# Second block's feed-forwards: normalised inputs of 256 columns from the fifth unit on, 112 bytes off the weights

## The reference, cut to what matters

```python
h = _modulate(_rmsnorm(x, ffn1_norm[l]), sh1, sc1)          # h * (1 + scale) + shift
x = x + FFN_RES * gt1[:, None, :] * _swiglu(h, ffn1_w_in[l], ffn1_w_out[l])
# _swiglu: a, b = split(h @ w_in); (silu(a) * b) @ w_out     D_FF = 2816
```

## Time and profile before

| | |
|---|---|
| median of 3 runs | 3090.3 us (3087.77 to 3093.15) |
| profiled execution, its own time | 3091.63 us |
| its span | 3089.9 us, mean granted clock 0.99 |
| PE / PEld / DVE / ACT / POOL busy | 97% / 87% / 68% / 31% / 23% |
| outer units of FF0 to FF3 | 134.0, 135.1, 133.9, 131.6 us |
| inner units of FF0 to FF3, first to last matmul's start | 63.7, 63.0, 63.5, 62.2 us |

### The profile page before, as it was taken

How to read it: one execution, slowest core, us unless ns; L and a number is a source line. 1 busy time by engine, 2 the same in 40 slices (tenths; PEclk the granted TensorE clock), 3 DMA queues, 4 the chain that set the end, 5 groups by cost and what they waited for, 6 DMA issues and landing times.

```text
span 3089.9 us, 45987 instructions
## 1 busy us (share of the span) xinstructions
PE 3001.7 (97%) x18914; PEld 2685.3 (87%) x18914; DVE 2103.8 (68%) x2247; ACT 971.1 (31%) x1027; POOL 703.3 (23%) x614
## 2 busy tenths in 40 slices
PE   8999999999999999999998899999999999999999
PEld 5778889988887888878888699899989999999999
DVE  4864359867279543795637776687797868768764
ACT  2112222212131121221215343343544343354443
POOL 1220100124113010130201022231462313228110
PEclk9999999999999999999999999999999999999999
DMA  7543235322245333353623387586547868755564
GB/s 266 191 150 96 95 87 200 137 96 82 96 127 192 126 94 103 123 204 109 204 99 123 107 268 251 172 279 225 200 158 247 258 204 274 239 188 198 158 188 154
DMA packets 501665, 522.74 MB, mean 169 GB/s; under 512 B 15732, under 2 KB 433830, under 8 KB 501478
## 3 DMA queue, kind: packets, MB, share of 16 engines
q1 hardware_dynamic: 498536, 513.76, 50.4%
q0 software_dynamic: 2944, 6.32, 1.0%
HBM read 518.97 MB, written 1.05 MB: 168 GB/s over the span
## 4 chain that ended last, share of the span: by engine, by line
PE 77%; DVE 15%; ACT 3%; issue 3%; DMA 2%; POOL 0%; SPq 0%; DVEq 0%; ACTq 0%
PE ps L2309 22%; PE ps L2396 15%; PE ps L2486 14%; PE ps L2337 7%; PE ps L2510 7%; DVE wl L1293 4%; DVE acc L1247 3%; PE ps L2374 2%; DVE lnp L1247 2%; ACT wh L864 2%; PE ps L2353 2%; PE ps L2423 1%; DVE mraw L1254 1%; PE ps L2757 1%; PE ps L2789 1%
## 5 line engine op out<-in xcount | busy, mean ns | idle before, releaser
L1293 DVE TENSOR_TENSOR wl<-wraw,wh 128x2048 fp32r<-128x2048 f32 x341 | 825.6, 2421 | 513.1 <-ACT wh L864 508.5
L864 ACT ACTIVATE wh<-wraw 128x2048 fp32r<-128x2048 f32 x341 | 652.7, 1914 | 904.1 <-PE ps L2396 380.0
L2309 PE MATMUL ps<-xh,wh 128*128 128x512 f32 (+1 forms) x1504 | 553.7, 368 | 15.6 <-DVE wl L1293 15.4
L2309 PE MATMUL ps<-xh,wl 128*128 128x512 f32 (+1 forms) x1504 | 549.7, 366 | 0.0
L2309 PE MATMUL ps<-xl,wh 128*128 128x512 f32 (+1 forms) x1504 | 549.4, 365 | 0.0
L2486 PE MATMUL ps<-xh,wh 128*128 128x258 f32 x1408 | 405.9, 288 | 10.9 <-DVE wl L1293 7.1
L704 POOL CAST hh<-ht 128x256 f32 (+1 forms) x176 | 143.5, 816 | 1170.0 <-DVE ht L1685 845.8
L2486 PE MATMUL ps<-xh,wl 128*128 128x258 f32 x1408 | 401.5, 285 | 0.0
L2486 PE MATMUL ps<-xl,wh 128*128 128x258 f32 x1408 | 400.5, 284 | 0.0
L1247 DVE SCALAR_TENSOR_TENSOR acc<-mraw,svec,acc 128x1024 f32<-128x1024 f32 x259 | 347.7, 1362 | 6.1 <-DVE prea L1332 0.4
L2309 PEld LDWEIGHTS ps<-xh,wh 128*128 128x128 f32 x1504 | 284.1, 189 | 63.4 <-DVE wl L1293 17.1
(11 more groups left out here) (443 smaller groups left out, 5456.3 us busy)
## 6 DMA issues: line engine op xcount, KB each, us to landing
wraw<-in_ffn_w_in SPq DMA_DIRECT2D x352, 512.0 KB, 4.8
wraw<-in_ffn_w_out SPq DMA_DIRECT2D x176, 512.0 KB, 4.2
mraw<-in_ada_w SPq DMA_DIRECT2D x72, 1024.0 KB, 6.3
mraw<-in_w_mod SPq DMA_DIRECT2D x64, 1024.0 KB, 6.7
wraw<-in_gmlp_w_in SPq DMA_DIRECT2D x48, 512.0 KB, 4.2
wraw<-in_mix_w_in SPq DMA_DIRECT2D x48, 512.0 KB, 4.5
wraw<-in_gmlp_w_out SPq DMA_DIRECT2D x24, 512.0 KB, 3.9
first_w<-in_w_mod SPq DMA_DIRECT2D x8, 1024.0 KB, 11.0
```

Of the source, the lines that this page charges most:

```text
L864: act.activation(wh[:, slot], wraw[:, slot], ACT.Copy).then_inc(whi_done, 1)
L1293: dve.tensor_tensor(wl[:, slot], wraw[:, slot], wh[:, slot].bitcast(F32), ALU.subtract)\
L2309: m = pe.matmul(ps[:, bank, 0:width], a, b, start=k == p == 0, stop=k == KD - 1 and p == 2)
```

## The change

From outer unit 4 on (`EARLY = 4`) the input is the finished one, (x * scale / rms) + shift, in new halves `yh` and `yl` of 256 columns, each chunk 1,024 bytes apart and 112 bytes past a multiple of 1,024. They are made in turns 0 to 2: eight `scaled` on DVE, eight `yh` on ACT, eight `low_scaled` on DVE. Turns 4 to 21 lose take(i) (three DVE instructions); SiLU and product read PSUM directly, and the banks are freed by the product, which stands behind the low half of unit i+2 in DVE's order. The hidden halves of all inner units lie 1,136 bytes in, also 112 bytes past a multiple of 1,024. `FF_MODS` moves its first eight pieces.

```diff
-INNER_AT = {5: 0, 6: 48, 8: 0, 9: 48, 11: 0}
-INNER_STEP = {5: 4, 6: 0, 8: 16, 9: 0, 11: 4}
+INNER_AT = {5: 0, 6: 284, 8: 284, 9: 284, 11: 284}
+INNER_STEP = {5: 0, 6: 0, 8: 0, 9: 0, 11: 0}
+EARLY = 4
-FF_MODS = (2, 4, 6, 8, 10, 12, 14, 16, 18, 20, 22, 24)
+FF_MODS = (5, 6, 7, 9, 11, 12, 14, 16, 18, 20, 22, 24)
...
+        yh, yl = (late_in[:, 28 + i * KD * T:28 + (i + 1) * KD * T].rearrange("p (k q) -> p k q", k=KD) for i in range(2))
...   ACT, turn i
+                            if i < EARLY:
+                                act.wait_ge(a_ready, EARLY * late(s) + i + 1)
+                            else:
+                                act.wait_ge(w_used, u0 + i + 1)
...
+                                act.activation(sg[:, pair, T:2 * T], ps[:, 2 * pair, 0:T], ACT.Silu).then_inc(sg_ready, 1)
+                        for n in range(4 * i, 4 * i + 4) if i < 2 else ():
+                            j = order_in(s)[n]
+                            act.wait_ge(y_scaled, 8 * late(s) + n + 1)
+                            act.activation(yh[:, j], sq[:, j], ACT.Identity, bias=modc[:, s["i"] % 2, 0, 0, j:j + 1]).then_inc(y_high, 1)
...   DVE
+                    def product_late(i):
+                        pair = i % 2
+                        dve.wait_ge(sg_ready, s["n_sg"] + i + 1)
+
+                        dve.wait_ge(h_ready, s["n_h"] + i)
+                        dve.tensor_tensor(ht[:, pair, 0:T], ps[:, 2 * pair + 1, 0:T], sg[:, pair, T:2 * T], ALU.mult).then_inc(hidden, 1)
+                        dve.wait_ge(hidden, KF * late(s) + i + 1)
+                        dve.sem_inc(pair_free, 1)
+                    def scaled(n):
+                        j = order_in(s)[n]
+                        dve.scalar_tensor_tensor(out=sq[:, j], in0=xT[:, j], scalar=prea[:, 0, j:j + 1], in1=rstd_b,
+                                                 op0=ALU.mult, op1=ALU.mult).then_inc(y_scaled, 1)
+                    def low_scaled(n):
+                        j = order_in(s)[n]
+                        dve.wait_ge(y_high, 8 * late(s) + n + 1)
+                        dve.scalar_tensor_tensor(out=yl[:, j], in0=sq[:, j], scalar=modc[:, s["i"] % 2, 0, 0, j:j + 1],
+                                                 in1=yh[:, j].bitcast(F32), op0=ALU.add, op1=ALU.subtract).then_inc(y_ready, 1)
...
-                        if 0 < i < KF:
+                        if 0 < i < EARLY:
                             take(i)
...
-                        if i < KF:
+                        if i < EARLY:
                             product(i)
+                        elif i < KF:
+                            product_late(i)
+                        for n in range(4 * i - 4, 4 * i) if i in (1, 2) else ():
+                            low_scaled(n)
+                        for n in range(4 * i, 4 * i + 4) if i < 2 else ():
+                            scaled(n)
...   PE
+                                if i == EARLY and r == 0:
+                                    pe.wait_ge(y_ready, 8 * late(s) + n + 1)
...
+                                width = XW if i < EARLY else T
+                                high, low = (w[:, k, 0:width] for w in (now if i < EARLY else (yh, yl)))
```

More of the change, by code:

```diff
@@ L240, in program @@
         q2, k2 = (w[:, 1].rearrange("p (a b) -> p a b", a=4) for w in (gate, acc))
+        _, late_in = alias(("before_late", [P, 2 * KD * XS], F32), ("late_in", [P, 28 + 2 * KD * T], F32R))
+        yh, yl = (late_in[:, 28 + i * KD * T:28 + (i + 1) * KD * T].rearrange("p (k q) -> p k q", k=KD) for i in range(2))
         sb("place_of_inputs", [P, 2 * KD * 2 * T])
@@ L343, in program @@
         sq_act, sq_pool, sq_summed = sem("sq_act"), sem("sq_pool"), sem("sq_summed")
+        y_scaled, y_high, y_ready = sem("y_scaled"), sem("y_high"), sem("y_ready")
         hidden, ss_ready, rb_ps, rb_ready, a_ready = sem("hidden"), sem("ss_ready"), sem("rb_ps"), sem("rb_ready"), sem("a_ready")
@@ L438, in inner_at, with late @@
             return bass.ds(idx * (T + half) + (INNER_AT[s["i"]] - j % 2 * half), T)
+        def late(s):
+            return (s["n_sg"] - subs[B2]["n_sg"]) // KF
         def ff_mods(idx):
@@ L950, in _ @@
                             pair = i % 2
-                            act.wait_ge(a_ready, b0 + i + 1)
+                            if i < EARLY:
+                                act.wait_ge(a_ready, EARLY * late(s) + i + 1)
+                            else:
+                                act.wait_ge(w_used, u0 + i + 1)
                             if b0 + i > 1:
                                 act.wait_ge(hidden, b0 + i - 1)
-                            act.activation(sg[:, pair, T:2 * T], sg[:, pair, 0:T], ACT.Silu, bias=shift_col[:, pair, 0:1])\
-                                .then_inc(sg_ready, 1)
+                            if i < EARLY:
+                                act.activation(sg[:, pair, T:2 * T], sg[:, pair, 0:T], ACT.Silu, bias=shift_col[:, pair, 0:1])\
+                                    .then_inc(sg_ready, 1)
+                            else:
+                                act.activation(sg[:, pair, T:2 * T], ps[:, 2 * pair, 0:T], ACT.Silu).then_inc(sg_ready, 1)
[3 more added lines that the diff above has]
+                            act.activation(yh[:, j], sq[:, j], ACT.Identity, bias=modc[:, s["i"] % 2, 0, 0, j:j + 1]).then_inc(y_high, 1)
                 elif s["kind"] == "ffn":
@@ L2483, in _ @@
                                     pe.wait_ge(lo_ready, 8 * s["m"] + n + 1)
+                                if i == EARLY and r == 0:
+                                    pe.wait_ge(y_ready, 8 * late(s) + n + 1)
                                 at = slice(k * CW + r * P, k * CW + (r + 1) * P)
-                                for p, (a, b) in enumerate(parts(wh[:, slot, at], wl[:, slot, at], now[0][:, k, 0:XW], now[1][:, k, 0:XW])):
-                                    m = pe.matmul(ps[:, 2 * pair + r, 0:XW], a, b, start=n == p == 0, stop=n == KD - 1 and p == 2)
+                                width = XW if i < EARLY else T
+                                high, low = (w[:, k, 0:width] for w in (now if i < EARLY else (yh, yl)))
+                                for p, (a, b) in enumerate(parts(wh[:, slot, at], wl[:, slot, at], high, low)):
+                                    m = pe.matmul(ps[:, 2 * pair + r, 0:width], a, b, start=n == p == 0, stop=n == KD - 1 and p == 2)
                             if i == 1 and r == 0:
```

## The result

The changed kernel takes 3181.61 us (median of 4 runs, 3177.3 to 3183.63), the kernel before 3089.81 (4 runs, 3087.77 to 3093.15): ratio 1.0294, 95% interval 1.0276 to 1.0312, slower by 91.8 us. The prediction was 3149 (3128 to 3172): right in direction and in where the waits stand, 33 us short in size and outside its range. The profiled execution took 3180.62 us, its span is 3178.9, its mean clock 0.979.

A forecast was written before the change was run, and what follows sets the result against it. PE's pace was taken to bound the kernel, then what makes PE wait. 3 x 22.5 (FF0 to FF2) - 2.4 (FF3) - 6.5 (inner units) = +58.6 us on 3090.3 gave 3149 us, range 3128 to 3172.

The forecast's parts named there:

- Part 1: Late outer units take 5.44 us instead of 5.77, 5.9 less a feed-forward; inner units together 6.5 us less.
- the two SBUF read ports: Weight loads take nothing from the running matmul, so place cannot matter: under 1 us gained a feed-forward, 3166 us; chance 0.02.
- Rival B: Matmuls at the new places run at the slow pace, 118 ns: 3162 us; chance 0.11.
- Part 2: Turns 4 to 21: banks freed behind the low half, 5.05 us after PE's end, under 5.44; costs nothing while DVE is on time.
- Part 3: Making the finished input in the first turns delays PE's start of unit 4 by 2.4 us, bounds 0 and 5.
- Part 4: FF0 to FF2: later pieces hold SP's unit loads; PE waits 10.1, 4.6, 2.7, 1.4, 4.6 and 2.0 us.
- The clock: Half clock after PE's long waits: 3 us more in each of FF0 to FF2, bounds 0 and 8; perhaps 1 in FF3.
- A: The forecast itself: late loads cost some 20 us of PE time in each of three feed-forwards; chance 0.70.
- C: SP isn't held and raw unit 8 lands before PE ends unit 6: faster, 3076 us; chance 0.07.
- D: Unit's halves overtake the piece, 5.5 instead of 8.1 us from issue; four holds shrink by 2.6: 3110 us; chance 0.07.
- E: A pair of transfers takes 9 us and half clock is paid after each wait: +9 each, 3176 us; chance 0.05.

The follow-up runs named there:

- The experiment: Changed kernel, at turn 21 alone the SiLU ahead of ACT's high half and the product ahead of DVE's low half: 3166.99 us, ratio 1.0259.
- the run with the shorter lots: Changed kernel with PE's waits filled by dummy matmuls, fewer than in a first try (40 instead of 65 ahead of unit 8): 3174.57 us, ratio 1.0271.

## Why the prediction came out short

**Part 1 (columns and place): right.** 5.44 us a unit at 112 bytes, in every plain unit. The inner halves' part was put at 6.5 us and measured, alone, 5.7 in the four feed-forwards; the 1.4 of sub 5 was not in the sum. The prediction had read out of the two SBUF read ports (the Trainium skill, TensorE: Matmul & The Clock Gate, Part 2) that the place could not matter. It does: the same matmul takes 113, 118 and 120 ns at three offsets, and offset 0 costs 20.6 us over the changed kernel. Whether it is the weight load beside the matmul that the place disturbs, no run here shows. Rival B had asked for a slow pace at 112 bytes, and there was none.

**Part 2 (the late product): the step that failed.** "It costs nothing while DVE is on time" followed only the outer units, where each pair of banks has 5.44 us to come free. The first inner unit needs unit 21's pair after 24 of its 48 matmuls, and there the product is always too late: 2.1 to 2.5 us of standing in all four feed-forwards, FF3 too, and a low clock behind it in three of them. The experiment gave 14.6 us back; the inner totals missed the forecast by 16.3 (9.8 more instead of 6.5 less), so this one wait is nearly half of the 33 us. It could be read in the kernel: `pair_free` had a second reader, and I had only asked who waits for it inside the loop that I was costing.

**Part 3 (making the input): right place, small by 1.2 us in FF1.** Four `low_scaled` and four `scaled` took 3.90 us, not 3.2: the price of 0.40 apiece, which the earlier trace rows with 0.52 does not show, held for `scaled` (four in 1.66 us) and not for `low_scaled` (four in 2.31). In turn 0 four `scaled` took 2.32 and not 1.6. PE began unit 4 3.1 us late in FF1 instead of 2.4, and unit 3, forecast as just in time, 0.5 late. The price of a clock level behind it (unit 4 takes 7.18 us) was not in the sum.

**Part 4 (the moved pieces): right, each stall a little short.** All of the stalls came, in the order named, and the part done alone cost 65 us. FF1 from unit to unit, by the prediction's own times and as measured:

| FF1 | predicted | measured | what made the difference |
|---|---|---|---|
| start to unit 7 | 47.4 | 49.1 | Part 3's 1.2; half clock in unit 4, 1.7; the first unit 1.1 shorter than before |
| 7 to 8 | 15.6 | 15.9 | |
| 8 to 10 | 15.5 | 17.0 | piece 3.1 instead of 2.6; pair of loads 9.1 instead of 8.1 |
| 10 to 11 | 8.2 | 9.05 | piece 3.15, and 0.2 between it and the product |
| 11 to 13 | 12.3 | 12.9 | |
| 13 to 15 | 15.5 | 15.8 | |
| 15 to 19 | 23.8 | 26.1 | half clock in unit 15, 1.7; the fold's wait 2.6 instead of 2.0 |
| 19 to inner | 16.3 | 18.1 | half clock in unit 19, 1.75 |

The sum is 154.6 + 3 for the clock against 164.0, 6.4 us short; FF0 is 9.1 short, FF2 2.6. (19.3 and 3 are 22.3; the prediction goes on with 22.5, which makes 0.6 us in its total.) The row of 8 to 10 can be read in SP and ACT of the kernel after, the issue of piece 3 and the landing of load(10):

```profile
2435.71 0.37 SPq L538 DMA_DIRECT2D mraw<-in_ada_w  x1
...
2444.80 1.91 ACT L872 ACTIVATE wh<-wraw 128x2048 fp32r<-128x2048 f32 x1 [11.83 <-DMA wraw<-in_ffn_w_in]
```

**The clock: 3 us was small for FF1.** I let the loss fall into the next wait, which is right up to unit 13, but counted only one of the others. Three stand in FF1 (units 4, 15 and 19, 5.2 us by the differences 7.18 and 7.19 less 5.44). In the run with the shorter lots 3.2 of them came back at the units themselves, and the 1.7 of unit 4 went into unit 8's late load; but FF1's outer units as a whole got only 1.1 us shorter and the median 7, so what the clock costs in all stays open.

So of the 33 us, some 16 stand in the inner units, nearly all of them Part 2's missed wait, and 19 in the outer units: in FF1, by the table, about 2 of the 6 are the clock, the rest the longer piece (0.5 us each), the longer pair of transfers and Part 3's 1.2; no run takes these apart. FF3's outer units gained 1.3 us instead of 2.4. Against the 35 stands the rest of the kernel, 5.0 us shorter in the two profiled executions, 1.4 of it in sub 5's inner units; these executions are 89.0 us apart where the medians are 91.8. Why FF0 lost 3 to 7 us more than its sisters I cannot say in full: its units 3, 4, 7 and 11 took 9.5, 8.5, 16.9 and 8.4 us, FF1's 8.9, 7.2, 15.9 and 5.6.

**The rivals.** A's mechanism holds. C (loads in time) is out: piece 2 and load(8) went out at 2419.82 and 2420.23, behind turn 5's piece. D (halves overtake the piece) is out: 7.9 us for the pair. E is the nearest in size, and half right: one pair took 9.1 us, and half clock was paid three times in FF1; but it was given 0.05 and lacked the bank wait as well. The range was too narrow because its bounds came from the sizes of terms already in the sum; a step put at nothing in all four feed-forwards had no upper end in it.

## What to carry to other kernels

When the instruction that frees a buffer moves, list every waiter of its semaphore in the whole program, the first user behind the loop too; here the loop itself had slack and the first user after it had none, at 4 us each. In a queue that is in order, moving work by a turn also moves the waits in front of everything behind it: DVE's work was the same and SP's order cost 57 us, so give the consumer's turn and the issue's place separate tables. A faster pace is only worth what its helpers let through: once the late waits were found one by one and all taken out, a change that lost 92 us gained 27.

## What was not expected of the hardware

- Where the moving operand starts, with the weights at multiples of 1,024 bytes, sets the pace of a 256-column matmul: 113 ns at 112 bytes, 120 ns at 0, and at 192 bytes either 118 or 113 from one stretch to the next, at a granted clock of 1.00 throughout.
- A dummy fp32 matmul of 128 columns took 0.226 us (65 of them 14.6 us at full clock), not the 0.127 assumed; the records show each twice.
- DVE's multiply-add over 1,024 columns takes 1.28 to 1.30 us alone, 1.45 when it starts just behind GpSimd's cast and 1.65 beside the subtraction, which in turn takes 1.51 us instead of 0.74. Which of the two is stretched depends on who starts first, by as little as 0.03 us.
